# Where a token factor is applied: VectorE at the PSUM bank instead of ahead of the matmuls

## The reference

```python
h = rms_norm(x, attn_norm)        # x * rsqrt(mean(x^2) + eps) * gain
proj = h @ w_in                   # 6,344 columns
(aq, ak, av, iq, ik, iw, bq, bf, bi, bg, cq, ckv, ckpe, gate_logits) = split(proj)
o_a = dsa_attention(aq, ak, av, iq, ik, iw, ...)   # indexer, top 64 of the keys, softmax
o_b = hgrn2_mixer(bq, bf, bi, bg, ...)             # recurrence in chunks
o_c = mla_attention(norm(cq) @ w_qb, norm(ckv) @ w_kvb, rope(ckpe))
x = x + (sigmoid(gate_logits) * (o_a, o_b, o_c) @ w_up) @ w_out
```

## Time and profile before

| | us |
|---|---|
| median of 3 runs | 1049.81 (1049.63 to 1050.15) |
| the profiled execution | 1050.89 |
| its span, first to last instruction | 1049.10 |
| PE busy in the span | 1038.7 |
| PEld busy | 1011.4 |
| DVE busy | 745.9 |
| ACT busy | 579.9 |

### The profile page before, as it was taken

The page is one execution under the profiler, slowest core; times in us unless marked ns, Lnnn a source line. Parts: engine busy times, 40 slices in busy tenths (PEclk is TensorE's granted clock), DMA queues, the critical chain, the costliest instruction groups (busy, mean ns, idle before and its releaser), DMA issues.

```text
span 1049.1 us, 22214 instructions
## 1 busy us (share of the span) xinstructions
PE 1038.7 (99%) x8760; PEld 1011.4 (96%) x8760; DVE 745.9 (71%) x1098; ACT 579.9 (55%) x880; POOL 77.7 (7%) x92
## 2 busy tenths in 40 slices
PE   9999999999999999999999999999999999999998
PEld 7999998999999999999999999898899999999998
DVE  6899998747876666657666667668977876665666
ACT  4556755576565554556544445455666665454453
POOL 0000000002310000111000001041001300000110
PEclk9999999999999999999999999999999999999999
DMA  6456523345455554665655456555435555564663
GB/s 220 148 182 210 201 97 111 124 158 200 169 195 200 200 200 142 202 205 181 221 184 191 152 192 217 181 181 182 140 121 201 194 183 191 195 209 140 195 228 121
DMA packets 32444, 187.81 MB, mean 179 GB/s; under 512 B 3832, under 2 KB 7552, under 8 KB 14720
## 3 DMA queue, kind: packets, MB, share of 16 engines
q1 hardware_dynamic: 31472, 185.58, 50.9%
q0 software_dynamic: 416, 1.06, 0.4%
q10 hardware_dynamic: 496, 0.33, 0.2%
HBM read 184.98 MB, written 1.06 MB: 177 GB/s over the span
## 4 chain that ended last, share of the span: by engine, by line
PE 83%; DVE 8%; ACT 2%; issue 1%; DMA 1%; DVEq 0%; ACTq 0%
PE acc L685 79%; DVE wlo L1579 3%; PE area_a L685 3%; PE area_t L685 2%; ACT whi L1183 1%; DMA raw<-in_w_qk 1%; DVE score L1809 1%; PE area_t L951 1%; DVE work L1822 0%; DVE st L1820 0%; DVE mask L1784 0%; ACT he L1183 0%; DVE st L1769 0%; ACT L1213 0%; DVE qk L1611 0%
## 5 line engine op out<-in xcount | busy, mean ns | idle before, releaser
L685 PE MATMUL acc<-hs,whi 128*128 128x256 f32 x3584 | 618.1, 278 | 1.7 <-DVE wlo L1579 1.1
L685 PEld LDWEIGHTS acc<-hs,whi 128*128 128x128 f32 x3584 | 539.2, 187 | 8.5 <-issue 4.5
L685 PE MATMUL acc<-hs,wlo 128*128 128x256 f32 x1792 | 495.0, 276 | 0.0
L1183 ACT ACTIVATE whi<-raw 128x1024 fp32r<-128x1024 f32 (+3 forms) x379 | 357.1, 978 | 168.3 <-PE acc L685 114.5
L1579 DVE TENSOR_TENSOR wlo<-raw,whi 128x1024 fp32r<-128x1024 f32 (+4 forms) x259 | 276.8, 1109 | 96.6 <-ACT whi L1183 95.5
L685 PEld LDWEIGHTS acc<-hs,wlo 128*128 128x128 f32 x1792 | 335.6, 187 | 0.2
L685 PE MATMUL acc<-hid,whi 128*128 128x256 f32 x1056 | 180.1, 276 | 0.4 <-DVE wlo L1579 0.3
L685 PEld LDWEIGHTS acc<-hid,whi 128*128 128x128 f32 x1056 | 159.2, 188 | 0.8 <-DVE wlo L1579 0.8
L685 PE MATMUL acc<-hid,wlo 128*128 128x256 f32 x528 | 145.8, 276 | 0.0
L1667 DVE TENSOR_TENSOR wlo<-raw,whi 128x1024 fp32r<-128x1024 f32 x120 | 141.2, 1218 | 4.7 <-ACT whi L1183 4.7
L1680 DVE TENSOR_TENSOR hbuf<-acc,sbuf 128x256 f32<-128x256 f32 x66 | 28.0, 424 | 114.0 <-PE acc L685 110.6
(11 more groups left out here) (316 smaller groups left out, 1028.2 us busy)
## 6 DMA issues: line engine op xcount, KB each, us to landing
raw<-in_w_gu SPq DMA_DIRECT2D x66, 1024.0 KB, 4.8
raw<-in_w_dn SPq DMA_DIRECT2D x48, 704.0 KB, 4.2
raw<-in_w_up SPq DMA_DIRECT2D x10, 1024.0 KB, 4.7
raw<-in_w_gates1b SPq DMA_DIRECT2D x8, 1024.0 KB, 4.8
raw<-in_w_out SPq DMA_DIRECT2D x8, 1024.0 KB, 4.8
raw<-in_w_qk SPq DMA_DIRECT2D x8, 1024.0 KB, 4.8
raw<-in_w_gates SPq DMA_DIRECT2D x8, 1024.0 KB, 4.7
raw<-in_w_projT_b SPq DMA_DIRECT2D x7, 1024.0 KB, 4.8
```

The source lines that it names most:

```text
L685: return nc.tensor.matmul(out, w, m, start=start, stop=stop, skip_group_check=True)
L1183: return nc.scalar.activation(out, in_, f, **kw)
```

## The change

The factor `xr` is no longer multiplied into x ahead of tile 0. `hs` becomes x * gain alone, split into high and low parts straight from x, and the factor is multiplied in afterwards. Blocks in transposed form take it as they leave the bank: kik, ak, cq, ckv, bf, bg and all 24 gate blocks in a VectorE tensor_tensor with `xr`, bq in a scalar_tensor_tensor; these 43 blocks leave `BY_SCALAR`. iq and aq stay ScalarE copies and get their factor later as a per-token column, in the relu of idx* and in dsa_s*. avw and bi are multiplied by a column where they were copied. A new step `column0` makes those columns (two small PE products, three small VectorE instructions). The order of the opening is rewritten, tile 0 runs block after block (`opening_tile`), `keep_warm` ahead of it goes from 6 to 2 products, the loads of tiles 2 and 3 are let go one half tile earlier, and the two DMAs that double the keys move from ScalarE's queue to SP's.

```diff
-    work("distances mask0 drel norm0 bias0 H1 L1")
-    work("0a 0b bound0 mask1 H2 L2")
-    work("1a 1b bias1 mask2 H3 L3")
+    work("distances mask0 drel norm0 bias0 H1 L1a bound0 mask1 L1b")
+    work("0a 0b H2 L2")
+    work("1a 1b mask2 column0 bias1 H3 L3")
...
-        BY_SCALAR = {BLOCKS[b] + k for b, c in (("kik", 1), ("iq", 4), ("projT_b", 14), ("bq", 4), ("bg", 4),
-                                                ("gates1a", 8), ("q_c", 6), ("kv_c", 4), ("gates1b", 16))
-                     for k in range(c)}
+        BY_SCALAR = {BLOCKS[b] + k for b, ks in (("iq", range(4)), ("projT_b", range(1, 5)), ("q_c", range(6)),
+                                                 ("kv_c", range(4))) for k in ks}
...
-                    load(a[name][i], g % 2, n, 2 * g - 2)
+                    load(a[name][i], g % 2, n, {2: 1, 3: 3}.get(g, 2 * g - 2))
+                if g == 3:
+                    sp.wait_ge(S("block_freed"), LEFT_PSUM[BLOCKS["kik"]][1])
+                    sp.dma_start(kpe[ROPE:P, :], kpe[0:ROPE, :]).then_inc(S("keys_doubled"), 16)
+                    sp.dma_start(ik[0:ROPE, :], ik[ROPE:P, :]).then_inc(S("keys_doubled"), 16)
...
+            def opening_tile():
+                for b in range(2):
+                    bank_free(b)
+                    half_ready(0, b)
+                    for k in range(KD):
+                        if b == 0:
+                            pe.wait_ge(S("hs_lo"), k + 1)
+                        c = (b * KD + k) * P
+                        m = one_region(acc[b], whi[:, 0, c:c + P], wlo[:, 0, c:c + P], hs[:, k, :],
+                                       k == 0, k == KD - 1)
+                    m.then_inc(S("block_done"), 1)
...
-                        keep_warm(BLOCKS["kik"], 6)
+                        keep_warm(BLOCKS["kik"], 2)
```

ScalarE's part of `norm0`:

```diff
-                split_high(0, 0)
+                act.wait_ge(S("vec_loaded"), 16)
+                for k in range(KD):
+                    if k == KD // 2:
+                        split_high(0, 0)
+                    fn(hs[:, k, 0:T], x[:, k, :], ACT.Copy, scale=late_gain(name, k)).then_inc(S("hs_hi"), 1)
+                split_high(0, 1)
                 act.wait_ge(S("t_full"), TURN_T[name] + 1)
                 rms_factor(xr[:], area_t[:, 0, :], D, "t_freed")
-                split_high(0, 1)
-                hs_high("h_value", 0, lambda k: tmp[:, k % 4, :])
```

VectorE's reading of a bank (`read_block`; the last two lines were there):

```diff
+                elif n == BLOCKS["kik"]:
+                    dve.wait_ge(S("t_freed"), TURN_T["norm0"] + 1)
+                    v.tensor_tensor(kpe[0:ROPE, :], bank[0:ROPE, 0:T], xr[0:ROPE, :], ALU.mult)
+                    v.tensor_tensor(ik[ROPE:P, :], bank[ROPE:P, 0:T], xr[ROPE:P, :], ALU.mult)\
+                        .then_inc(S("block_freed"), 1)
+                elif n - BLOCKS["bq"] in range(B_H):
+                    v.scalar_tensor_tensor(SUM_DEST[n], bank[:, 0:T], float(P) ** -0.5, xr[:], ALU.mult, ALU.mult)\
+                        .then_inc(S("block_freed"), 1)
                 elif n in SUM_DEST and n < BLOCKS["pgp"] + 8:
                     v.tensor_tensor(SUM_DEST[n], bank[:, 0:T], xr[:], ALU.mult).then_inc(S("block_freed"), 1)
```

VectorE's part of `norm0`:

```diff
+            def first_low(k):
+                dve.wait_ge(S("hs_hi"), k + 1)
+                v.scalar_tensor_tensor(hs[:, k, T:2 * T], x[:, k, :], late_gain("norm0", k),
+                                       hs[:, k, 0:T].bitcast(F32), ALU.mult, ALU.subtract).then_inc(S("hs_lo"), 1)
...
-                split_low(0, 0)
-                dve.wait_ge(S("t_freed"), TURN_T[name] + 1)
                 dve.wait_ge(S("vec_loaded"), 16)
-                for k in range(KD):
-                    if k == 2:
-                        split_low(0, 1)
-                    if k >= 2:
-                        hs_low(name, k - 2, tmp[:, (k - 2) % 4, :])
-                    v.scalar_tensor_tensor(tmp[:, k % 4, :], x[:, k, :], vec[:, g + k:g + k + 1], xr[:],
-                                           ALU.mult, ALU.mult).then_inc(S("h_value"), 1)
-                for k in (KD - 2, KD - 1):
-                    hs_low(name, k, tmp[:, k % 4, :])
+                for k in range(KD):
+                    if k == KD // 2:
+                        split_low(0, 0)
+                    first_low(k)
+                split_low(0, 1)
```

More of the change, by code:

```diff
@@ L749, in square_sums, with factor_column @@
                 m.then_inc(S("t_full"), 1)
-            def factor_column():
-                pe.wait_ge(S("factor_made"), 1)
-                t = take_t("column4")
+            def factor_column(step):
+                if step == "column4":
+                    pe.wait_ge(S("factor_made"), 1)
+                else:
+                    pe.wait_ge(S("con_loaded"), 16)
+                t = take_t(step)
                 for tt in range(NT):
@@ L780, in tile @@
                 if (g in HS_BEFORE or g in MS_BEFORE) and name != "w_fvl":
-                    if part == 0:
+                    if part == 0 and g == 0:
+                        opening_tile()
+                    elif part == 0:
                         first_tile(g, first_of[name][0])
@@ L1006, in step @@
                     if name == "bias0":
-                        keep_warm(BLOCKS["kik"], 6)
+                        keep_warm(BLOCKS["kik"], 2)
+                elif name == "column0":
+                    factor_column(name)
                 elif name in NORMS:
@@ L1263, in tile @@
                         residual_used(n - 1)
-                    if n == BLOCKS["kik"]:
+                    if n in BY_SCALAR:
                         act.wait_ge(S("block_done"), n + 1)
[L1266 to L1274, removed]
+                        fn(SUM_DEST[n], acc[n % 4][:, 0:T], ACT.Copy).then_inc(S("copied"), 1)
                 if g == FIRST["w_pg"] + 3 and part:
@@ L1406, in step @@
                 elif name == "input_squares":
-                    act.wait_ge(S("copied"), LEFT_PSUM[BLOCKS["projT_b"] + 9][1])
+                    act.wait_ge(S("block_freed"), LEFT_PSUM[BLOCKS["projT_b"] + 9][1])
                     act.wait_ge(S("sines"), 2)
@@ L1444, in step @@
                 elif name == "decay_xa":
-                    act.wait_ge(S("copied"), LEFT_PSUM[BLOCKS["projT_b"] + 13][1])
+                    act.wait_ge(S("block_freed"), LEFT_PSUM[BLOCKS["projT_b"] + 13][1])
                     act.wait_ge(S("decay_space"), 1)
@@ L1468, in step @@
                     load_set(SILUS)
-                    act.wait_ge(S("copied"), LEFT_PSUM[BLOCKS["bg"] + 3][1])
+                    act.wait_ge(S("block_freed"), LEFT_PSUM[BLOCKS["bg"] + 3][1])
                     fn(flat(bg[:, :, :]), flat(bg[:, :, :]), ACT.Silu).then_inc(S("hgrn_gate"), 1)
@@ L1483, in step @@
                         ("gates2", 8 * b + 7)
-                    by, count = LEFT_PSUM[BLOCKS[last[0]] + last[1]]
+                    n = BLOCKS[last[0]] + last[1]
+                    by, count = LEFT_PSUM[n]
                     act.wait_ge(S(by), count)
@@ L1620, in read_block @@
                     tt = n - BLOCKS["avw"]
[L1621 to L1622 removed]
+                    c = st[:, 106 + tt:107 + tt]
+                    v.tensor_scalar(av[:, tt, :], bank[:, 0:P], c, None, ALU.mult)
+                    v.tensor_scalar(iw[:, tt, :], bank[:, P:AVW], c, None, ALU.mult).then_inc(S("block_freed"), 1)
                 elif n - BLOCKS["fvl"] == 2:
@@ L1637, in read_block @@
                 else:
[L1638 to L1642, removed]
-                    else:
-                        raise AssertionError(n)
+                    tt = n - BLOCKS["bi"]
+                    if tt in (0, 1):
+                        v.tensor_scalar(bi[:, tt, :], bank[:, :], st[:, 106 + tt:107 + tt], None, ALU.mult)\
+                            .then_inc(S("block_freed"), 1)
+                    else:
+                        assert n - BLOCKS["kv_c"] in (4, 5)
+                        v.tensor_copy(vc[:, n - BLOCKS["kv_c"] - 4, :], bank[:, :]).then_inc(S("block_freed"), 1)
             def tile(g, part):
@@ L1718, in _, with factor_columns @@
             HS_ORDER = ("norm0", "norm1", "norm2", "norm4", "norm5", "norm6")
[L1720 to L1723, removed]
+            def first_low(k):
+                dve.wait_ge(S("hs_hi"), k + 1)
+                v.scalar_tensor_tensor(hs[:, k, T:2 * T], x[:, k, :], late_gain("norm0", k),
+                                       hs[:, k, 0:T].bitcast(F32), ALU.mult, ALU.subtract).then_inc(S("hs_lo"), 1)
+            def factor_columns():
+                dve.wait_ge(S("t_full"), TURN_T["column0"] + 1)
+                v.tensor_copy(st[:, 106:106 + NT], area_t[:, 0, 0:NT]).then_inc(S("t_freed"), 1)
+                dve.wait_ge(S("t_freed"), TURN_T["column0"] + 1)
+                v.tensor_scalar(st[:, 108:108 + NT], st[:, 106:106 + NT], IDX_D ** -0.5 * IDX_H ** -0.5, None, ALU.mult)
+                v.tensor_scalar(st[:, 110:110 + NT], st[:, 106:106 + NT], float(P) ** -0.5, None, ALU.mult)\
+                    .then_inc(S("columns_scaled"), 1)
```

(5 more changed lines are left out.)

17 lines of the change are left out of this document (7 added, 10 removed).

## The result

| | before | changed |
|---|---|---|
| median, us | 1049.81 (1049.63 to 1050.15) | 1054.07 (1053.27 to 1054.54) |
| the profiled execution | 1050.89 | 1053.91 |
| its span | 1049.10 | 1052.1 |

What follows compares the result with a forecast made beforehand. PE's list of matmuls plus its waits was taken to bound the kernel, with VectorE full from 42.4 to 93 us. Terms -2.2 + 3.4 + 1.7 = +2.9 us on the median gave 1052.7 us, range 1049.0 to 1055.4.

Steps and rivals of the forecast that it cites:

- The opening: Start to the bias step: PE starts earlier, waits 0.8 us for tile 2, and gains 2.2 us.
- The reads up to tile 12: Tiles 4 to 12: ten more VectorE reads and the avw multiplications, 3.63 us in a full queue, delay PE by 3.4.
- 0.2 us of room: At tile 12: slack between the end of VectorE's split and PE's product, subtracted from the delay.
- The price: Each VectorE bank read with xr costs 0.335 us behind another, not its full 0.42 as by the drain rule.
- The later reads: From 93 to 155 us: 16 more reads, 5.5 us, mostly hidden; PE loses 1.7 us, at hk and qn.
- VectorE's 5.0 us of waits: From 93 to 155 us: VectorE's waits for ScalarE's splits and exponentials hide most of the 5.5 us of reads.
- The last 16 reads: From 155 us on: 5.4 us of gate reads lie in 24 us of VectorE idle time and cost nothing.
- The covers: Key doubling, the relu's wait for columns and SP's load stay hidden; uncovered, up to the 4.8 us of a load.
- Profile and median: Whole kernel: terms are differences inside the span, so their sum is added to the median, 1049.81 us.
- Rival A: Tiles 9 to 12: VectorE's queue has room for the reads, only the opening counts; 1047.6 or 1046.8 us, chance 0.14.
- Rival B: Opening: tile 2 lands at 23.4 as before, no gain, reads paid in full; 1054.9 us, chance 0.15.

Runs made afterwards that it cites:

- e5: Changed kernel with ten instructions more: VectorE reads each bank of ak, cq, ckv and bf once more with the factor, into scratch; 1057.35 us.
- e3: Changed kernel, but the 16 blocks bq, bg and gates1a leave the bank by ScalarE's plain copies, factor left out; 1051.68 us.
- e4: Changed kernel, but the 16 gates1b blocks leave the bank by ScalarE's plain copies, factor left out; 1054.87 us.
- e1: Changed kernel, but all 42 blocks behind kik leave the bank by ScalarE's plain copies, factor left out; 1048.0 us, ratio 0.9983 to before.
- e2: Changed kernel, but the ten blocks ak, cq, ckv and bf leave the bank by ScalarE's plain copies, factor left out; 1050.87 us.
- v6: Changed kernel reordered: ScalarE's sines and function loads behind its splits of tile 4, VectorE's mask4 ahead of the avw reads; 1053.1 us.
- v3: v1 with ScalarE also reading avw and bi, the column as its scale; 1054.81 us.
- v7: v5b reordered: each rebuilt chunk pair cut into two steps, idx00's relu ahead of the last copies; 1047.34 us, ratio 0.9975 to before.
- v1: Changed kernel, but 26 blocks (ak to gates1a) leave by ScalarE's copies and GpSimd multiplies the factor in afterwards; 1055.51 us, ratio 1.0053 to before.
- v5: Changed kernel, but x * gain * xr is rebuilt for tiles from 4 on, their blocks leave by ScalarE's plain copies, sines moved; 1053.85 us.
- v5b: v5 with ScalarE also reading avw, the column as its scale; 1053.07 us.

## Why the prediction was right, and where it was short

The sign and the mechanism are as forecast, and so are the places but for one; the size was 2.9 us, measured are 3.9 in the traces and 4.3 in the medians.

- *The opening.* Forecast -2.2 with PE at 14.3, tile 2 split from 21.0, block 1b at 23.5 and the bias step at 26.6; the rows say 14.26, 21.14, 23.51 and 26.71. The gain at tile 2 is 2.0 us.
- *The reads up to tile 12.* Forecast +3.4, tile 12 at 94.3; the row says 94.83, +3.70 from tile 2. The sum of 3.63 us for VectorE was right: its split of tile 4 starts at 40.60, 1.84 us sooner than before (42.44), and its split of tile 12 1.81 us later, which makes 3.65. The step that failed is the start: the sum gave VectorE the 2.2 us of PE's lead, while VectorE entered the stretch with 1.84, behind ScalarE's split of tile 4; and of the 0.2 us of room between VectorE and PE only 0.11 was there (1.47 us from split to product before, 1.36 now).
- *The price.* 0.335 against 0.42 was settled by e5: 0.325. The Trainium skill's rule that was weighed ("VectorE: DVE Perf Modes", section "The DRAIN you can't avoid") says that the next instruction does not start until the pipe is empty, which would have been the 0.42; the same section adds that a next instruction that is not held starts earlier, which the prediction left out, and these runs agree with that.
- *The later reads.* Forecast +1.7 by two places, hk 0.7 and qn 1.0; measured +2.16 by three: hk 0.59 with what builds up on the way, tile 20 0.79, qn 0.78. The term that was missed is tile 20's split: I had counted on VectorE's 5.0 us of waits in this stretch and on two places where it runs short, and did not follow its queue to every split behind the gates1a reads. That all but 0.19 us of it comes from these reads is shown by e3.
- *The last 16 reads.* Forecast nothing; e4 agrees.
- *The covers.* The doubling of the keys, the relu's wait for the columns and SP's load show nowhere among PE's waits; the wait for relu_l (0.8, before 0.3) is there in e1 too, so it does not come from the reads. The prediction did not have it, but up to tile 12 the changed kernel's PE is held by VectorE's splits anyway.
- *Profile and median.* That the terms are added to the median was right. The spans alone, 3.0 us apart, would have seemed to confirm 2.9, but the first profile of before was long by 1.0 us behind all of this. The medians hold something more that the prediction did not have. Of the changed kernel's six executions four have a mean granted clock of 1.000 and took 1053.27 to 1054.23 us; two have 0.998 and took 1054.52 and 1054.54. In e2, e4 and v6 the executions at 0.998 are the longer ones too, by 1.0 to 1.3 us between the medians of the two groups; in e5 and v3 they are not. Before, e1, e3 and v7, in which PE waits 1.3 us for qn and not 2.0 to 2.2, have none at 0.998. In v1's trace, also 0.998, the clock was granted at 0.50 for 3.4 us right behind the wait for qn, and the lag grew by 0.9 us. So the longer wait for qn seems to have a second price in some executions; that it was this wait in those without a trace is not shown.

Rival A was right in its mechanism's price (e1: 1048.0, forecast 1047.6), and wrong in its condition: VectorE had no room. Rival B's cause did not come; tile 2 landed by 21.14. Its time, 1054.9, was near for another reason.

## What to carry to other kernels

An engine that is busy 71% of the span can be full for 50 us of it; the price of an instruction that is moved onto it is its start-to-start time wherever that engine has no wait before the bottleneck next needs it, and nothing only where such a wait takes it up: from 93 to 155 us VectorE had 5.0 us of waits, and 2.0 of the 5.5 us of reads still reached PE. Follow the receiving engine's queue to each place where the bottleneck takes something from it, and start from that engine's own lead, not from the bottleneck's. If work must move to it, move it to where it waits: here the same factor, applied once per chunk ahead of the full stretch instead of once per block inside it, turned a loss of 4.3 us into a gain of 2.5.

## What the runs showed of the hardware

- GpSimd and VectorE disturb each other only in some instructions: with GpSimd multiplying two SBUF tiles in v1, VectorE's subtraction of two SBUF tiles took up to 2.90 instead of 2.36 us per pair, four tensor_scalar of hk 1.92 instead of 1.14, and GpSimd's own up to four times its 0.74 (2.92 at 99.9 us), while MAX8 and MATCH_REPLACE8 stayed at 0.43 and 0.41.
- A short stand of PE can cost more than itself. In v5, behind a stand of 2.16 us that ended at 37.62, the clock was granted at half for 10.2 us and 4.8 us were lost; in v5b, behind 2.11 us, for 6.8 us; in v1, behind 2.21 us at qn, for 3.4 us; in e5, behind 1.84 us at tile 10, for 3.4 us, where VectorE's queue held PE anyway. Behind the 2.06 us at qn in the changed kernel's trace the clock stayed at 1.00, and so it did in v3 behind the same 2.21 us at qn as in v1. What tells these apart was not tried.
